# Five edits to a two-block transformer kernel: operand share-out of a chunked recurrence, query order, split sums, constants

## Chip, cores and metric

One core of one Trainium2 chip runs the whole kernel as one program. The metric is device time in microseconds (us) of an execution; three executions of the kernel before gave 2816.89, 2823.05 and 2823.09 us, median 2823.05 us. The core has a matrix engine (TensorE, PE), three elementwise engines (VectorE or DVE, ScalarE or ACT, GpSimd or POOL) and SyncE (SP), which here issues the weight transfers. The engines run side by side and meet at semaphores.

## What is computed

The input is 512 tokens of width 1024. The first block is one hybrid layer, the second has two layers of feed-forward, mixer, feed-forward. Cut to what the change touches:

```python
# first block
h = rms_norm(x, mix_pre_norm) * (1 + sc_m) + sh_m
proj = h @ w_in                       # c_q, c_kv, index keys | r, k, v, decay, a, gate
cq, ckv = rms_norm(c_q, q_norm), rms_norm(c_kv, kv_norm)
y_att = dsa_attention(...)            # causal, 8 heads, top 128 of the latent keys, plus rel. bias
# rwkv7_group, state S (64 x 64) per head, 8 heads, one step per token:
sa = einsum('bhij,bhj->bhi', S, a_t)
S = S * w_t[:, :, None, :] + sa[..., None] * b_t[:, :, None, :] + v_t[..., None] * k_t[:, :, None, :]
y_t = einsum('bhij,bhj->bhi', S, r_t)
x = x + g_m * rms_norm(concat([y_att, y_rwkv]) @ w_out, mix_post_norm)
hf = rms_norm(x, ffn_pre_norm) * (1 + sc_f) + sh_f
x = x + g_f * rms_norm((silu(hf @ w_ffn_gate) * (hf @ w_ffn_up)) @ w_ffn_down, ffn_post_norm)
# second block, two layers
h = h + 0.5 * swiglu(rms_norm_2(h, ...))
h = h + pool_fox_mixer(...)           # layer 0: attention of 8 heads with a forget decay
h = h + mla_mixer(...)                # layer 1: attention of 16 heads, chunk-causal
h = h + 0.5 * swiglu(rms_norm_2(h, ...))
```

Everything is fp32. A dense product is made as three passes over operands that are split into a high and a low part.

## The kernel before

**Stages.** The program is a row of stages, each a block with one instruction list per engine; all engines meet at a stage's end, and POOL then clears the semaphores of that stage (L800) before its own first work of the next. The order is: start; input products (`linear_stage` called with name "inproj", L1626 on); for each of two rounds a recurrence preparation (`rwkv_prep_stage`, L2315) and a recurrence chunk stage (`rwkv_chunk_stage`, L2457); the latent front; attention "dsa"; output product; feed-forward 1 and 2; inputs of the second mixer; attention "fox"; three stages with feed-forwards 3 and 4; attention "mla"; the last feed-forward. Weights come in 1 MB chunks through a ring that SP fills. 97% of the span TensorE is busy, most of it in the dense products.

**Constants.** `keep_clock(pe, bank, n)` (L158) issues n products of the constant identity whose result nobody reads. They stand where TensorE would otherwise wait.

**Input products.** Tiles of 512 tokens by 128 features, 8 pairs of k each (24 products, L748 and L750). Before tile 3, 4, 5, ... a callback puts small work between the tiles: `sums` (L1674) before tile 4 makes column sums of the squares of c_q, c_kv and index keys, 128x1 products from line L782, then four transposes (L1679). ScalarE takes roots of them, and `spread_latents` before tile 5 (L1694) uses those.

**Recurrence.** A round handles two head pairs, called groups 0 and 1. The sequence is cut into 8 chunks of 64. `R.W[g]` are 17 working tiles of 128x512 for each group (`nt, T, TT, X, A, B, K, KH, BH, RT, vt, kht, bht, at, akt, rk, rb`), which the trace names by where they lie (`spare`, `h`, `y`). The preparation stage makes the decays' exponentials on ScalarE, then products of them: on DVE for each group A, B, K and RT (L2448 to L2451), then a copy of the chunk ends (L2452); on POOL KH and BH (L2409, L2410). Its TensorE list ends in products of the adaLN weights (L928), a turn of their rows (L916) and `keep_clock(..., 7)` (14 records of the trace). Its ScalarE list ends in two sigmoids of the gate (round 0 alone).

The chunk stage inverts a triangular 64x64 matrix per chunk by doubling, levels s = 2, 4, 8, 16, 32. `group_steps` lists the steps of one group; the two groups' lists are interleaved. A step is 16 or 32 small products (L2549) and then evacuations on DVE or ScalarE; step n of TensorE waits for all evacuations of the steps up to n-2. Evacuations on DVE: a masked copy of a bank (L2489), `plus_one` (L2496, both inputs in SBUF), `turn` (L2493, a transpose), and the addition of a bank (L2512). The chain of a level is the product nt x T, masked copy X, the product TT x X, addition to T, turn to TT. Into it are put the `extra` steps, which need only the operands: transposes of V, KH, BH, A, then the products K x A, B x RT, K x RT and akt x vt:

```python
            for s in LEVELS[1:]:
                put(full(W.nt, W.T, 0), [("dve", masked(W.X, 0, f"low{s}"))])
                if extra:
                    out.append(extra.pop(0))
```

**Attention** (`attention_stage`, L2116) serves dsa, fox and mla. An item is a head h and a query block i of 128 queries; its scores are (i + 1) x 128 wide. `items` runs over head pairs, in each over the blocks falling (3, 2, 1, 0), in each over the two heads. TensorE works pair of items j: scores of pair j (L2148, in fox also the decay product L2154), transposes of the probabilities of pair j-2 (L2163), products with the values of pair j-3 (L2176 or L782), and `keep_clock(..., 3)` at j = 2 and 3. DVE reduces the scores with the bias or mask (L2206), negates the maximum (L2209), takes the reciprocal and scales (L2218); ScalarE makes the exponentials and copies the transposed probabilities (L2236). In dsa alone POOL makes bias plus mask for each item (L2296, L2295).

**Feed-forwards 1 and 2.** `first_chunks` (L1119) starts with `keep_clock` of 10 or 8 while DVE makes the first features.

## Time and profile before

| | before |
|---|---|
| runs | 2816.89, 2823.05, 2823.09 us |
| profiled execution, own time | 2815.81 us |
| its span | 2814.0 us |
| mean granted clock of TensorE | 0.991 |
| TensorE busy | 2716.2 us, 97%, 16250 instructions |
| VectorE busy | 1312.9 us, 47% |
| ScalarE busy | 847.7 us, 30% |
| GpSimd busy | 563.3 us, 20%, 387 instructions |
| DMA | 248.24 MB, mean 88 GB/s |

The profiled execution's own time is 1.81 us over its span. Times within it are counted from the span's start. In a row of the timeline the first number is the start, the second the length of the group of instructions, and what stands in brackets is the idle time of the engine ahead of it with what ended it. A TensorE row's length holds the drain of its last product, which overlaps the row after it.

### The profile page before, as it was taken

Reading aid. Unit: us, or ns where it says so; the run is one execution under the profiler, and the core shown is the slowest. Engines: PE = TensorE matmul, PEld = TensorE weight load, DVE = VectorE, ACT = ScalarE, POOL = GpSimd, SP = SyncE. Lnnn points to the kernel's source line nnn. Section 1 sums busy time; section 2 is a strip of 40 time slices with the busy share of each in tenths; the row PEclk is TensorE's granted clock in tenths of the full one; section 3 lists DMA queues with packets and bytes.
Section 4 is the critical chain, followed back from the end, with each engine's and each line's share of the span. In section 5 each row is a group of like instructions: output and inputs, shape, how many; then the busy total and the mean of one; then the engine's idle time right before and its main releaser. Section 6 shows DMA issues by size and latency. Waiting matters only on the chain. (4 is left out here: it accounts for less than half of the span.)

```text
span 2814.0 us, 38779 instructions
## 1 busy us (share of the span) xinstructions
PE 2716.2 (97%) x16250; PEld 2175.1 (77%) x16250; DVE 1312.9 (47%) x1851; ACT 847.7 (30%) x1269; POOL 563.3 (20%) x387
## 2 busy tenths in 40 slices
PE   7989898999999999999999999999999999999998
PEld 5868746778888788888868888888888746888886
DVE  3555678453323643335355434354343566543433
ACT  3232135522212421223263212232221347421222
POOL 2000123411212221114101211122021100130202
PEclk9999989999999999999999999999999999999999
DMA  9151210223232233323213232232322240333221
GB/s 291 51 166 48 78 37 5 62 95 98 92 103 84 90 96 98 97 78 107 75 31 105 91 103 92 84 111 91 104 90 90 53 105 1 103 94 104 92 92 42
DMA packets 256942, 248.24 MB, mean 88 GB/s; under 512 B 25972, under 2 KB 252088, under 8 KB 256640
## 3 DMA queue, kind: packets, MB, share of 16 engines
q1 hardware_dynamic: 256562, 245.70, 28.0%
q8 instruction: 129, 2.11, 0.3%
q14 instruction: 45, 0.37, 0.0%
q10 hardware_dynamic: 206, 0.06, 0.0%
HBM read 241.52 MB, written 2.12 MB: 87 GB/s over the span
## 5 line engine op out<-in xcount | busy, mean ns | idle before, releaser
L537 DVE TENSOR_TENSOR dense_wt_lo<-ring,dense_wt_hi 128x2048 fp32r<-128x2048 f32 (+1 forms) x177 | 437.0, 2469 | 290.2 <-ACT dense_wt_hi L522 290.2
L522 ACT CAST dense_wt_hi<-ring 128x2048 fp32r<-128x2048 f32 (+1 forms) x177 | 328.2, 1854 | 758.7 <-PE bank L764 752.7
L1276 POOL TENSOR_TENSOR dense_act_hi<-dense_act,const 128x512 fp32r<-128x512 f32 x110 | 212.9, 1936 | 1306.6 <-DVE dense_act L1268 1306.6
L764 PE MATMUL bank<-feat_hi,dense_wt_hi 128*128 128x512 f32 x1344 | 414.6, 390 | 0.0
L764 PE MATMUL bank<-feat_hi,dense_wt_lo 128*128 128x512 f32 x1344 | 413.8, 389 | 0.0
L764 PE MATMUL bank<-feat_lo,dense_wt_hi 128*128 128x512 f32 x1344 | 413.7, 389 | 0.0
L764 PEld LDWEIGHTS bank<-feat_hi,dense_wt_hi 128*128 128x128 f32 x1344 | 252.3, 188 | 53.3 <-issue 1.0
L764 PEld LDWEIGHTS bank<-feat_hi,dense_wt_lo 128*128 128x128 f32 x1344 | 252.3, 188 | 52.4
L764 PEld LDWEIGHTS bank<-feat_lo,dense_wt_hi 128*128 128x128 f32 x1344 | 252.3, 188 | 52.4
L764 PE MATMUL bank<-dense_act_hi,dense_wt_hi 128*128 128x512 f32 x912 | 281.5, 390 | 1.0 <-POOL dense_act_lo L1278 1.0
L764 PE MATMUL bank<-dense_act_hi,dense_wt_lo 128*128 128x512 f32 x912 | 280.8, 389 | 0.0
L764 PE MATMUL bank<-dense_act_lo,dense_wt_hi 128*128 128x512 f32 x912 | 280.8, 389 | 0.0
L764 PEld LDWEIGHTS bank<-dense_act_hi,dense_wt_hi 128*128 128x128 f32 x912 | 170.6, 188 | 38.4 <-POOL dense_act_lo L1278 3.1
L764 PEld LDWEIGHTS bank<-dense_act_lo,dense_wt_hi 128*128 128x128 f32 x912 | 171.2, 188 | 35.6
L764 PEld LDWEIGHTS bank<-dense_act_hi,dense_wt_lo 128*128 128x128 f32 x912 | 171.2, 188 | 35.6
L1268 DVE TENSOR_TENSOR dense_act<-dense_silu,bank 128x512 f32<-128x512 f32 x110 | 70.7, 684 | 259.6 <-PE bank L764 258.6
L1243 DVE SCALAR_TENSOR_TENSOR x<-bank,x 128x512 f32<-128x512 f32 x96 | 61.9, 686 | 234.1 <-PE bank L764 234.1
L1197 ACT ACTIVATE dense_silu<-dense_silu 128x512 f32<-128x512 f32 x88 | 54.1, 632 | 384.9 <-DVE dense_silu L1255 384.9
L1255 DVE TENSOR_TENSOR dense_silu<-bank,rs 128x512 f32<-128x512 f32 x86 | 55.4, 686 | 224.3 <-PE bank L764 223.9
L1278 POOL TENSOR_TENSOR dense_act_lo<-dense_act,dense_act_hi 128x512 fp32r<-128x512 f32 x110 | 153.4, 1395 | 16.3 <-issue 0.9
L277 POOL TENSOR_TENSOR h<-h 128x512 f32<-128x512 f32 x30 | 39.2, 1306 | 405.6 <-ACT h L262 404.5
L764 PE MATMUL bank<-last_feat_hi,dense_wt_hi 128*128 128x512 f32 x352 | 108.8, 390 | 0.0
(631 smaller groups left out, 3805.4 us busy)
## 6 DMA issues: line engine op xcount, KB each, us to landing
ring<-in_ffn_w_gate SPq DMA_DIRECT2D x44, 1024.0 KB, 5.4
ring<-in_ffn_w_up SPq DMA_DIRECT2D x44, 1024.0 KB, 5.4
ring<-in_ffn_w_down SPq DMA_DIRECT2D x32, 1024.0 KB, 5.0
ring<-in_ada_w SPq DMA_DIRECT2D x24, 1024.0 KB, 8.3
ring<-in_ffn_w_down SPq DMA_DIRECT2D x16, 768.0 KB, 4.2
ring<-in_w_ffn_gate SPq DMA_DIRECT2D x11, 1024.0 KB, 5.4
ring<-in_w_ffn_up SPq DMA_DIRECT2D x11, 1024.0 KB, 5.4
ring<-in_w_in SPq DMA_DIRECT2D x8, 1024.0 KB, 6.3
```

The costliest lines, as they stand in the source:

```text
L277: K.nc.gpsimd.tensor_tensor(K.h[:, 0, :], K.h[:, 0, :], K.h[:, k, :], ALU.add)
L522: self.nc.scalar.copy(self.wh[:, n % 2, 0:words], K.ring[:, n % RING, 0:words]).then_inc(K.high_done, 1)
L537: self.nc.vector.tensor_tensor(self.wl[:, n % 2, 0:words], K.ring[:, n % RING, 0:words], self.wh[:, n % 2, 0:words].bitcast(F32), ALU.subt ...
L764: lasts[m] = pe.matmul(outs[m], a, b, start=n == 0 and p == 0, stop=end and p == 2)
L1197: nc.scalar.activation(g[:, m, :], g[:, m, :], ACT.Silu).then_inc(s_silu, 1)
L1243: v.scalar_tensor_tensor(to, bank, 0.5, to, ALU.mult, ALU.add).then_inc(s_free, 1)
L1255: v.tensor_tensor(g[:, m, :], g[:, m, :] if post and c == 0 else K.bank[m][:, :], K.rs[:, :], ALU.mult).then_inc(s_gate, 1)
L1268: v.tensor_tensor(a[:, m, :], g[:, m, :], K.bank[2 + m][:, :], ALU.mult).then_inc(s_act, 1)
L1276: nc.gpsimd.tensor_tensor(ah[:, f, :], a[:, i % 2, :], K.k("ones")[:, 0:1].broadcast_to([P, T]), ALU.mult)
L1278: nc.gpsimd.tensor_tensor(al[:, f, :], a[:, i % 2, :], ah[:, f, :].bitcast(F32), ALU.subtract).then_inc(s_al, 1)
```

## The change

1. `first_chunks` (L1122): 12 constants in place of 10 (feed-forward 1), and 14 in place of 8 (feed-forward 2).
2. Input products: `sums` keeps the 8 column products of the squares of c_q, before tile 4; a new function `more_sums` does the other 8 and the four transposes, in the middle of tile 4, after 4 of its 8 pairs of k.
3. `attention_stage`: the first head pair takes its query blocks rising (0, 1, 2, 3); all others fall as before. All three attentions.
4. Recurrence. KH and BH are made by POOL at the start of the chunk stage (both KH, then both BH), with a new semaphore `s_hat` on which TensorE waits ahead of their transposes. The preparation has no POOL work left. K and RT are made by DVE in level 4 of the chunk stage, K after the masked copy, RT after the turn. The exponentials are kept for that in tiles rk, rb and akt. The `extra` steps stand in another order: V and A directly after the first two pairs of steps, KH at the end of level 2, BH at the end of level 4, and the four products in levels 8 and 16. The two sigmoids of the gate are moved to the start of ScalarE's list of the chunk stage.
5. The end of the preparation has `keep_clock(..., 2)` in place of 7.

```diff
-            K.keep_clock(pe, K.bank[0], 10 if mix else 8)
+            K.keep_clock(pe, K.bank[0], 12 if mix else 14)
...
-                product3(pe, bank_of(t), tiles[t][4](S, pe, w, t == 0)).then_inc(K.tiles_done, 1)
+                pairs = list(tiles[t][4](S, pe, w, t == 0))
+                if t in extra.get("mid_tensor", {}):
+                    product3(pe, bank_of(t), pairs[:4], stop=False)
+                    extra["mid_tensor"][t]()
+                    product3(pe, bank_of(t), pairs[4:], start=False).then_inc(K.tiles_done, 1)
+                    continue
+                product3(pe, bank_of(t), pairs).then_inc(K.tiles_done, 1)
...
     def sums():
         pe.wait_ge(box["sq"], 4)
-        for at, tiles_in in ((0, (0, 1)), (4, (2,)), (8, (3,))):
+        for b in range(TB):
+            product(pe, K.bank[7][:, b:b + 1], [(sq[n][:, b * P:(b + 1) * P], K.k("ones")[:, 0:1]) for n in (0, 1)])
+
+    def more_sums():
+        for at, tiles_in in ((4, (2,)), (8, (3,))):
...
-    items = [(h + e, i) for h in range(0, H, 2) for i in reversed(range(TB)) for e in range(2)]
+    items = [(h + e, i) for h in range(0, H, 2) for i in (reversed(range(TB)) if h else range(TB)) for e in range(2)]
...
-                K.keep_clock(pe, K.bank[1], 7)
+                K.keep_clock(pe, K.bank[1], 2)
...
-                if rnd == 0:
-                    nc.scalar.activation(M.g[:, :], M.g[:, :], ACT.Sigmoid)
-                    nc.scalar.activation(M.g2[:, :], M.g2[:, :], ACT.Sigmoid)
 
             @block.gpsimd
             def _(pool):
-                for e in range(2):
-                    pool.wait_ge(s_keys, e + 1)
-                    pool.wait_ge(s_exp, 4 * e + 4)
-                    nc.gpsimd.tensor_tensor(W[e].KH, key(e), W[e].TT, ALU.mult)
-                    nc.gpsimd.tensor_tensor(W[e].BH, W[e].bht, W[e].TT, ALU.mult)
+                pass
...
                     v.tensor_tensor(W[e].A, W[e].at, W[e].T, ALU.mult)
-                    v.tensor_tensor(W[e].B, W[e].bht, W[e].nt, ALU.mult)
-                    v.tensor_tensor(W[e].K, key(e), W[e].nt, ALU.mult)
-                    v.tensor_tensor(W[e].RT, M.rkv[:, p, :], W[e].X, ALU.mult)
-                    v.tensor_copy(R.end[:, e, :], chunks(W[e].X)[:, :, C - 1])
+                    v.tensor_tensor(W[e].B, W[e].bht, W[e].rk, ALU.mult)
+                    v.tensor_copy(R.end[:, e, :], chunks(W[e].rb)[:, :, C - 1])
...
-            for src, dst in ((V, W.vt), (W.KH, W.kht), (W.BH, W.bht), (W.A, W.at)):
+            for src, dst in ((V, W.vt), (W.A, W.at), (W.KH, W.kht), (W.BH, W.bht)):
...
+            out.append(extra.pop(0))
+            out.append(extra.pop(0))
             for s in LEVELS[1:]:
-                put(full(W.nt, W.T, 0), [("dve", masked(W.X, 0, f"low{s}"))])
-                if extra:
+                late = []
+                if s == 4:
+                    late = [("dve", lambda: v.tensor_tensor(W.K, key, W.rk, ALU.mult)),
+                            ("dve", lambda: v.tensor_tensor(W.RT, query, W.rb, ALU.mult))]
+                put(full(W.nt, W.T, 0), [("dve", masked(W.X, 0, f"low{s}"))] + late[0:1])
+                if s in (8, 16):
                     out.append(extra.pop(0))
...
+        hat = {2 * at + g: 2 * m + g + 1 for m, at in enumerate((6, 9)) for g in range(2)}
...
+                    if n in hat:
+                        pe.wait_ge(s_hat, hat[n])
...
             def _(pool):
+                for e, W in enumerate(R.W):
+                    nc.gpsimd.tensor_tensor(W.KH, M.rkv[:, 4 + ps[e], :], W.akt, ALU.mult).then_inc(s_hat, 1)
+                for W in R.W:
+                    nc.gpsimd.tensor_tensor(W.BH, W.bht, W.akt, ALU.mult).then_inc(s_hat, 1)
                 pool.wait_ge(s_pe, n_A)
...
             def _(act):
+                if rnd == 0:
+                    nc.scalar.activation(M.g[:, :], M.g[:, :], ACT.Sigmoid)
+                    nc.scalar.activation(M.g2[:, :], M.g2[:, :], ACT.Sigmoid)
```

Lines shift: after the change the small products of the chunk stage are L2560, the masked copies L2491, the turns L2495, `plus_one` L2498, the attention's scores L2159 and transposes L2174.

**Order on POOL, preparation and chunk stage of the first round.** L2409 and L2410 are KH and BH of the kernel before; L800 are the clears. Before:

```order
L800 ISA x27
L2404 UNCONDITIONAL_BRANCH
L2409 TENSOR_TENSOR spare<-rkv,spare 128x512
L2410 TENSOR_TENSOR spare<-spare 128x512
L2409 TENSOR_TENSOR spare<-rkv,y 128x512
L2410 TENSOR_TENSOR spare<-h,y 128x512
L2329 UNCONDITIONAL_BRANCH
L800 ISA x17
L2568 UNCONDITIONAL_BRANCH
L2572 TENSOR_TENSOR spare<-const,end 128x512 x2
```

And with the change, where L2582 is KH and L2584 BH:

```order
L800 ISA x27
L2412 UNCONDITIONAL_BRANCH
L800 ISA x16
L2579 UNCONDITIONAL_BRANCH
L2582 TENSOR_TENSOR spare<-rkv,spare 128x512
L2582 TENSOR_TENSOR spare<-rkv,h 128x512
L2584 TENSOR_TENSOR spare<-spare 128x512
L2584 TENSOR_TENSOR spare<-h 128x512
L2587 TENSOR_TENSOR spare<-const,end 128x512 x2
```

The four products stand behind the branch into the chunk stage and behind its clears (L800), no longer ahead of them.

**Order on DVE, level 4 of the chunk stage of the first round.** L2489 (L2491) is the masked copy, L2512 (L2520) the addition to T, L2493 (L2495) the turn; `spare` and `h` or `y` are groups 0 and 1. Before:

```order
L2489 TENSOR_TENSOR spare<-bank,const 128x512
L2489 TENSOR_TENSOR y<-bank,const 128x512
L2512 TENSOR_TENSOR spare<-bank,spare 128x512
L2493 STREAM_TRANSPOSE spare<-spare 128x512
L2512 TENSOR_TENSOR h<-bank,h 128x512
L2493 STREAM_TRANSPOSE y<-h 128x512
```

With the change, L2514 is K and L2515 RT:

```order
L2491 TENSOR_TENSOR spare<-bank,const 128x512
L2514 TENSOR_TENSOR spare<-rkv,spare 128x512
L2491 TENSOR_TENSOR y<-bank,const 128x512
L2514 TENSOR_TENSOR spare<-rkv,y 128x512
L2520 TENSOR_TENSOR spare<-bank,spare 128x512
L2495 STREAM_TRANSPOSE spare<-spare 128x512
L2515 TENSOR_TENSOR spare<-rkv,spare 128x512
L2520 TENSOR_TENSOR h<-bank,h 128x512
L2495 STREAM_TRANSPOSE y<-h 128x512
L2515 TENSOR_TENSOR h<-rkv,y 128x512
```

Each masked copy is now followed by a K, and each turn by an RT, before the other group's evacuation comes to its turn.

**Order on TensorE, start of the attention mla.** L2148 (L2159) are scores, L2163 (L2174) transposes, L2176 (L2187) products with the values, L158 constants. Before:

```order
L2148 MATMUL bank<-mK,mQ 128x512 x2
L2148 MATMUL bank<-mK,mQ 128x384 x2
L2148 MATMUL bank<-mK,mQ 128x256 x2
L158 MATMUL bank<-const 128x128 x3
L2163 MATMUL bank<-const,mla_S 128x128 x8
L2148 MATMUL bank<-mK,mQ 128x128 x2
L158 MATMUL bank<-const 128x128 x3
L2163 MATMUL bank<-const,mla_S 128x128 x6
L2176 MATMUL bank<-mla_pt,mV 64x128 x8
L2148 MATMUL bank<-mK,mQ 128x512 x2
```

With the change:

```order
L2159 MATMUL bank<-mK,mQ 128x128 x2
L2159 MATMUL bank<-mK,mQ 128x256 x2
L2159 MATMUL bank<-mK,mQ 128x384 x2
L158 MATMUL bank<-const 128x128 x3
L2174 MATMUL bank<-const,mla_S 128x128 x2
L2159 MATMUL bank<-mK,mQ 128x512 x2
L158 MATMUL bank<-const 128x128 x3
L2174 MATMUL bank<-const,mla_S 128x128 x4
L2187 MATMUL bank<-mla_pt,mV 64x128 x2
L2159 MATMUL bank<-mK,mQ 128x512 x2
L2174 MATMUL bank<-const,mla_S 128x128 x6
```

The first transposes are 2 in place of 8, and the widest items of the first head pair stand next to those of the second.

## Rows read from the trace of the kernel before

**Rows 1.** the page, busy time of each engine.

```profile
PE 2716.2 (97%) x16250; PEld 2175.1 (77%) x16250; DVE 1312.9 (47%) x1851; ACT 847.7 (30%) x1269; POOL 563.3 (20%) x387
```

**Rows 2.** view of waits, TensorE: us in total, times, longest us.

```profile
PE bank L2549 <- DVE spare L2493: 7.8, 10, 1.5
...
PE bank L2163 <- ACT mla_pt L2236: 4.5, 15, 0.8
PE bank L2163 <- ACT fox_pt L2236: 4.3, 7, 0.7
```

**Rows 3.** timeline of TensorE, start stage and input products.

```profile
34.47 1.95 PE L782 MATMUL bank<-const,h 128*128 128x1 f32 x16 [0.25 <-POOL h L195]
...
74.50 2.74 PE L782 MATMUL bank<-const,y 128*128 128x1 f32 x24
...
79.43 0.63 PE L748 MATMUL bank<-inproj__feat_lo,inproj_wt_hi 128*128 128x512 f32 x1
...
82.84 0.39 PE L748 MATMUL bank<-inproj__feat_hi,inproj_wt_hi 128*128 128x512 f32 x1
83.06 0.39 PE L748 MATMUL bank<-inproj__feat_lo,inproj_wt_hi 128*128 128x512 f32 x1
```

**Rows 4.** windows: us, busy times and counts by engine, PEclk, DMA share, GB/s.

```profile
80.00:84.00 4.00, 4.00 (x14) 3.16 (x13) 0.00 (x0) 0.00 (x0) 0.00 (x0) 0.65 0.00 0
...
202.00:206.00 4.00, 3.90 (x80) 3.91 (x82) 1.42 (x3) 0.30 (x1) 0.00 (x0) 0.57 0.02 4
```

**Rows 5.** timeline of DVE, end of the first preparation stage.

```profile
187.08 1.75 DVE L2449 TENSOR_TENSOR spare<-spare 128x512 f32<-128x512 f32 x1
...
190.44 0.68 DVE L2451 TENSOR_TENSOR spare<-rkv,spare 128x512 f32<-128x512 f32 x1
...
193.60 0.16 DVE L959 TENSOR_TENSOR mod<-bank,par 128x16 f32<-128x16 f32 x1
```

**Rows 6.** timeline of TensorE, into the first chunk stage.

```profile
189.53 1.18 PE L916 MATMUL bank<-const,rprep_row 128*128 128x1 f32 x8
190.57 1.81 PE L158 MATMUL bank<-const 128*128 128x128 f32 x14
194.14 4.07 PE L2549 MATMUL bank<-spare 64*64 64x64 f32 x128 [1.76 <-PEq L2329]
199.72 1.15 PE L2549 MATMUL bank<-spare 64*64 64x64 f32 x32 [1.51 <-DVE spare L2493]
202.09 1.85 PE L2549 MATMUL bank<-h 64*64 64x64 f32 x32 [1.23 <-DVE y L2493]
```

**Rows 7.** timeline of POOL, same stretch.

```profile
184.89 1.72 POOL L2410 TENSOR_TENSOR spare<-spare 128x512 f32<-128x512 f32 x1
```

**Rows 8.** timeline of attention dsa: TensorE, POOL, DVE.

```profile
442.11 3.25 PE L2148 MATMUL bank<-ckv,h 128*128 128x512 f32 x8 [2.08 <-PEq L1885]
...
443.66 5.92 POOL L2296 TENSOR_TENSOR dsa_bm<-rkv,mask 128x512 f32<-128x512 f32 x6 [30.56 <-issue]
...
465.15 2.62 POOL L2296 TENSOR_TENSOR dsa_bm<-rkv,mask 128x512 f32<-128x512 f32 x2 [1.63 <-DVE dsa_stat L2209]
...
462.88 0.92 DVE L2218 TENSOR_SCALAR dsa_S<-dsa_S,dsa_stat 128x512 f32<-128x512 f32 x2
...
465.21 2.77 DVE L2218 TENSOR_SCALAR dsa_S<-dsa_S,dsa_stat 128x384 f32<-128x384 f32 x2
```

**Rows 9.** timeline of DVE, first chunk stage.

```profile
198.17 0.69 DVE L2496 TENSOR_TENSOR spare<-spare,const 128x512 f32<-128x512 f32 x1
```

**Rows 10.** timeline of TensorE, start of attention mla.

```profile
2302.28 1.09 PE L2163 MATMUL bank<-const,mla_S 128*128 128x128 f32 x8 [0.52 <-DVE mla_S L2218]
...
2305.30 1.00 PE L2163 MATMUL bank<-const,mla_S 128*128 128x128 f32 x6 [0.81 <-ACT mla_pt L2236]
```

**Rows 11.** timeline of TensorE, starts of feed-forwards 1 and 2.

```profile
563.36 0.70 PE L774 MATMUL bank<-feat_hi,dense_wt_hi 128*128 128x512 f32 x2 [1.17 <-DVE feat_lo L478]
...
939.77 1.19 PE L774 MATMUL bank<-feat_hi,dense_wt_hi 128*128 128x512 f32 x2 [2.30 <-DVE feat_lo L665]
```

More of the change, by code:

```diff
@@ L1792, in in_proj_stage @@
                  extra={"sems": sems, "box": box, "sync": sync, "before": before, "helper": helper, "pool": on_pool,
+                        "mid_tensor": {4: more_sums},
                         "at_tensor": {3: ik_product, 4: sums, 5: spread_latents, 6: spread_ik, 7: lambda: dots(0), 8: lambda: dots(1)},
@@ L2323, in rwkv_prep_stage @@
         root, oka = st.sb("root", [P, 2, 8]), st.sb("oka", [P, 2])
-        s_w, s_lora, s_dots, s_sig, s_kk, s_sq, s_norm, s_root, s_inv, s_spread, s_l, s_exp, s_keys = st.sems(
-            "w", "lora", "dots", "sigmoid", "kk", "square", "norm", "root", "inverse", "spread", "logs", "exp", "keys")
+        s_w, s_lora, s_dots, s_sig, s_kk, s_sq, s_norm, s_root, s_inv, s_spread, s_l, s_exp = st.sems(
+            "w", "lora", "dots", "sigmoid", "kk", "square", "norm", "root", "inverse", "spread", "logs", "exp")
         key = lambda e: M.rkv[:, 4 + ps[e], :]
@@ L2357, in _ @@
                     for b in range(TB):
-                        last = pe.matmul(K.bank[4 * e + 3][:, 2 * b:2 * b + 2], W[e].akt[:, b * P:(b + 1) * P], pick, start=True, stop=True)
+                        last = pe.matmul(K.bank[4 * e + 3][:, 2 * b:2 * b + 2], W[e].X[:, b * P:(b + 1) * P], pick, start=True, stop=True)
                     last.then_inc(s_norm, 1)
@@ L2377, in _ @@
                     act.wait_ge(s_kk, e + 1)
-                    nc.scalar.activation(W[e].akt, W[e].at, ACT.Square).then_inc(s_sq, 1)
+                    nc.scalar.activation(W[e].X, W[e].at, ACT.Square).then_inc(s_sq, 1)
                 mod.row_out(act, at)
@@ L2394, in _ @@
                     nc.scalar.activation(W[e].T, W[e].T, ACT.Exp).then_inc(s_exp, 1)
[L2395 to L2397 removed]
+                    nc.scalar.activation(W[e].rk, W[e].kht, ACT.Exp, scale=-1.0).then_inc(s_exp, 1)
+                    nc.scalar.activation(W[e].rb, W[e].kht, ACT.Exp).then_inc(s_exp, 1)
+                    nc.scalar.activation(W[e].akt, W[e].akt, ACT.Exp).then_inc(s_exp, 1)
                 for r in range(at + 3, at + 8):
                     mod.row_out(act, r)
[L2400 to L2402 removed]
             @block.gpsimd
             def _(pool):
[L2406 to L2410 removed]
+                pass
             @block.vector
@@ L2419, in _ @@
                 for e in range(2):
-                    lw, L, eA, eC = W[e].vt, W[e].kht, W[e].T, W[e].TT
+                    lw, L, eA, eC = W[e].vt, W[e].kht, W[e].T, W[e].akt
                     dve.wait_ge(s_sig, 2 * e + 1)
@@ L2444, in _ @@
                     v.scalar_tensor_tensor(W[e].bht, W[e].at, -1.0, W[e].bht, ALU.mult, ALU.mult)
-                    dve.drain().then_inc(s_keys, 1)
+                dve.drain()
                 for e, p in enumerate(ps):
@@ L2463, in rwkv_chunk_stage @@
         S = st.sb("state", [P, 2, 2, HD])
-        s_pe, s_dve, s_act, s_sp, s_sv, s_diag = st.sems("products", "vector_out", "scalar_out", "state_product", "state", "diagonal")
+        s_pe, s_dve, s_act, s_sp, s_sv, s_diag, s_hat = st.sems("products", "vector_out", "scalar_out", "state_product", "state", "diagonal", "scaled_to_end")
         v, a = nc.vector, nc.scalar
@@ L2469, in group_steps @@
             W, b0 = R.W[g], 4 * g
-            V = M.rkv[:, 8 + ps[g], :]
+            V, key, query = M.rkv[:, 8 + ps[g], :], M.rkv[:, 4 + ps[g], :], M.rkv[:, ps[g], :]
             bank = lambda n: K.bank[b0 + n][:, :]
@@ L2506, in group_steps @@
             extra.append((g, full(W.akt, W.vt, 3), [("act", lambda: a.copy(W.akt, bank(3)))]))
+            out.append(extra.pop(0))
+            out.append(extra.pop(0))
             for s in LEVELS[1:]:
-                put(full(W.nt, W.T, 0), [("dve", masked(W.X, 0, f"low{s}"))])
-                if extra:
+                late = []
[4 more added lines that the diff above has]
+                if s in (8, 16):
                     out.append(extra.pop(0))
                 if s != LEVELS[-1]:
-                    put(full(W.TT, W.X, 1), [("dve", lambda: v.tensor_tensor(W.T, bank(1), W.T, ALU.add)), ("drain", None), ("dve", turn(W.TT, W.T))])
+                    put(full(W.TT, W.X, 1), [("dve", lambda: v.tensor_tensor(W.T, bank(1), W.T, ALU.add)), ("drain", None), ("dve", turn(W.TT, W.T))] + late[1:2])
                 else:
                     put(full(W.X, W.TT, 2), [("dve", lambda: v.tensor_tensor(W.TT, bank(2), W.TT, ALU.add))])
-                if extra:
+                if s != LEVELS[-1]:
                     out.append(extra.pop(0))
```

3 lines of the change are left out of this document (removed).

## The prediction

> **What bounds the kernel now.** I read the page first: TensorE is busy 2716.2 of 2814.0 us [rows 1], so only time in which it stands still or runs slowly can be had, some 98 us in all. The view of TensorE's waits comes second. The two places that the change rewrites are there: in the recurrence's chunk stage it waits 7.8 us in 10 waits for a tile of DVE, in the attentions 4.5 us in 15 waits (mla) and 4.3 us in 7 (fox) for ScalarE's copies of the probabilities [rows 2]. Third, the timeline of TensorE at each edited place, with the granted clock by windows, and last DVE and POOL at the same times. The change is hence five small terms, each some us of 2820.
>
> **The base.** The profiled execution's own time is 2815.81 us, near the lowest of the three runs (2816.89, 2823.05, 2823.09); its span is 2814.0. Those four executions have a mean of 2819.7, and I set the sum against that. 0.3% of the median, 8.5 us, is about what a measurement can tell from no change.
>
> **Input products.** Ahead of tile 4 stands an unbroken run of one-column products, from 74.50 to the next dense product. From 79.43 to 82.84 eight dense products start 0.43 us apart, and from there 0.22 [rows 3]; the clock granted in that window is 0.65 as a mean [rows 4], so the lower of the two levels, 1.2 GHz, came behind the run. That costs 8 x 0.2 = 1.6 us. A shorter run of 1.95 us at 34.47 had no such fall behind it. The change leaves runs of about 1.8 and 2.3 us with 12 dense products (2.7 us) between. I take the fall as gone and pay one more break between dense and narrow work, 0.4: **-1.2**. Ends: -1.6, and +0.4 if the clock falls all the same. The roots on ScalarE begin some 2.7 us later; they need to be back for the callback ahead of tile 5, with 12 dense products behind the sums instead of 24, and this hides them, by a narrow margin; if not, TensorE waits under 1 us there.
>
> **End of the preparation.** The chunk stage starts on TensorE at 194.14; DVE had ended with the adaLN addition at 193.60 + 0.16 [rows 5, 6]. DVE's B takes 1.75 while POOL's product (1.72) runs, and 0.68 when POOL is done [rows 5, 7]. With POOL's four products and DVE's K and RT gone, DVE is no longer last: A and B for both groups and two small copies are under 3 us from 185.6. Next late is TensorE itself: the turn at 189.53 is followed by constants at 190.57 [rows 6], of which a few (0.7 us) stay, so it ends near 191.25 and the new stage starts 0.35 later, as now, at 191.6. That is -2.55 a round, **-5.1** for two. The constants dropped cost nothing, they lay under DVE's work; kept, they would now stand on the path. The two sigmoids move off ScalarE's end; in the chunk stage its first copy, of V, is wanted only after the first DVE evacuations, so they lie beside other work.
>
> **K and RT on DVE.** Four operations of 0.68 us [rows 5] come into level 4 of each round, where TensorE already waits for DVE [rows 2]. K stands ahead of the other group's masked copy and RT ahead of its addition to T; of the four, two are on the chain from one group's step to the next: 2 x 0.65 = 1.3 a round, **+2.6**. Ends: 0 and +5.4.
>
> **POOL at the start of the chunk stage.** POOL first clears the sixteen semaphores of the preparation. In dsa, with 22 to clear, its first product came at 443.66, 1.55 after TensorE's first at 442.11 [rows 8]; here I take 1.55 x 16/22 = 1.1. It then holds four products of about 1.7 [rows 7], to some 8 us after the stage's start. In that time DVE does both `plus_one`, 0.69 alone [rows 9], with both inputs in SBUF. By the pair 0.68 and 1.75 [rows 5] that is up to +1.07 each. Group 1's is partly covered by group 0's products, so I take 0.9 a round, **+1.8**; ends 0 and +4.3. KH is wanted only after level 2 and BH after level 4, later than POOL has them, so the two new waits on `s_hat` cost nothing. The new V and A steps behind the first two pairs do not fill the first pause: step n waits for all evacuations up to n-2, and V of group 0 has ahead of it the turn of group 0.
>
> The Trainium skill ("SBUF — State Buffer", section Who interferes with whom) says that a DVE instruction with two SBUF inputs contends with a GpSimd one that reads SBUF, and that whoever issues first blocks the other fully, not in part. By it `plus_one` would wait out a POOL product or slip in ahead of it. It speaks against this part of the change, and the trace agrees in size (1.75 beside 1.72). By the pair of rows this term is +1.8; by the rule, an estimate, each round costs between 0 (`plus_one` gets in first) and 1.7 (it waits out one product), so 0 to +3.4 and a sum of -7.6 to -4.2.
>
> **Clock in the chunk stage.** The pauses behind the first steps are 1.51 and 1.23 [rows 6]. The clock of 202 to 206 was 0.57 in round 1 [rows 4], and a row of 32 products took 1.85 there against 1.15 at 199.72 [rows 6]. The longer pauses (about 2.4 and 1.4) can bring such a fall in both rounds and for longer: 0 to +2.1, I take the middle, **+1.0**. The recurrence together: -5.1 + 2.6 + 1.8 + 1.0 = **+0.3**.
>
> **Attentions.** With the first head pair rising, the first softmax is of 128 columns and no longer 512. In mla the fill has pauses of 0.52 and 0.81 [rows 10], and the first period two of 0.3 [rows 2], 1.9 in all. A pause costs more than its bracket: the row ahead counts the drain of its last product (0.39 long, the next 0.22 later [rows 3]), 0.17 for each of four. 2.6 in all, less one pause of 0.4 that I expect to stay where two blocks of 512 meet: **-2.2**. The work inside is the same, only later. Fox: a like fill (1.3), two waits of 0.61 [rows 2], the drains 0.7, less 0.6 that stays: **-2.6**. Ends for each: 0 and -3.8. In dsa another engine paces it: DVE's scaling takes 2.77 for two tiles of 384 while POOL's bias of 2.62 runs, and 0.92 for two of 512 without [rows 8]. POOL starts at 443.66 whatever the order. What is saved in the fill waits there again: **-0.1**, ends 0 and -2.7.
>
> **Constants of feed-forwards 1 and 2.** TensorE waits 1.17 and 2.30 for the first feature there [rows 11]. Two calls more (0.2) and six more (0.7) lie under those: **0**. The higher clock that they may keep is eaten by DVE's pace of features, for which TensorE waits anyway. Were the cover gone, they would cost 0.9.
>
> **Sum.** -1.2 + 0.3 - 0.1 - 2.2 - 2.6 + 0 = -5.8. On 2819.7 that is **2813.9**; on the profiled time 2810.0, on the median 2817.3.
>
> **Rivals.**
> 1. *The attention's gain is absorbed* as in dsa: the long blocks of heads 0 and 1 now meet those of 2 and 3, and DVE gets behind by what the fill had saved. For it: DVE and ScalarE, not TensorE, end the waits [rows 2]. Against: in mla the pauses in the steady part are only 0.3. Sum -1.2 + 0.3 - 0.1 = -1.0, so 2818.7. Chance 0.22.
> 2. *Everything pays.* POOL and DVE miss each other, K and RT fall into DVE's idle time, no clock falls (recurrence -5.1), in-proj -1.6, dsa -2.7, the others as above: -14.2, 2805.5; with a partial overlap 2805 to 2810. For it: DVE is busy only 47%. Against: in level 4 it is just what TensorE waits for. Chance 0.2.
> 3. *The slower side: POOL meets K and RT.* If POOL starts late or takes longer than 1.7, its last BH still runs when DVE comes to level 4. Then the four take 1.75 in place of 0.68, on the path +4.3 a round on top of the 1.3, and both `plus_one` the full 1.07, and BH is late for TensorE as well. Recurrence: -5.1 + 2 x (1.3 + 4.3 + 2.1 + 1.0) = +12.3. With the attention's gain 2826.2, without 2831. It decides from the point at which POOL's last product ends after DVE's first K. Against: 8 us after a start at 191.6 is before any level 4 (about 204). Chance 0.08.
> 4. *It does not do what it says*: the two runs of sums still halve the clock. That is inside the range, +1.6.
>
> **How the numbers follow.** Forecast 0.5 (own range 2809 to 2819, a bit over half of it below 2814.6, the 0.3% bound), rival 1 0.22, rival 2 0.2, rival 3 0.08. Faster by over 0.3%: 0.26 + 0.19 = 0.45. Slower by over 0.3% (above 2831.5): half of rival 3 and a rest, 0.05. Within 0.3%: 0.50. The range, 2805 to 2822, holds the forecast, rival 1 and most of rival 2, and leaves out rival 3 and the lowest part of rival 2.
>
> **What would show it.** Right: dense products of tile 4 at 0.22 throughout; the chunk stage's first TensorE row about 2.5 earlier than the preparation's own work would place it now; `plus_one` of group 0 longer than 1.5; a wait for the masked copy or addition in level 4; second head pair's first scores of mla 3 us earlier against the stage's start, the whole stage 2 to 3 shorter; dsa no shorter. Wrong: fox and mla of the same length (rival 1); `plus_one` at 0.69 and level 4 without a wait (rival 2); K or RT over 1.2 us (rival 3).

## The result, and the profile after

The change made the kernel slower. Its four executions gave 2835.26 to 2840.66 us, median 2837.61; the kernel before, with one further execution, has a median of 2821.26. The ratio is 1.0049, with a 95% interval of 1.0032 to 1.0066, some 14 us (9 to 19). The forecast was 2813.9 with a range of 2805 to 2822. Of all executions below only one stands apart, 5859.54 us in e7 beside eleven others of 2810.39 to 2828.53; e7's median of 2816.77 counts it (2816.46 without it), its ratio does not, and its cause is not known.

The page of the changed kernel, span and busy times [rows 1]:

```profile
span 2838.8 us, 38774 instructions
...
PE 2733.3 (96%) x16246; PEld 2189.0 (77%) x16246; DVE 1307.3 (46%) x1851; ACT 848.9 (30%) x1269; POOL 558.7 (20%) x387
```

TensorE is busy 17 us longer with hardly more work to do, and the span is 25 us longer. That is more than the 14 us by the ratio: this trace is of the slowest of the four executions (2840.66), and the one of before is of a fast one (2815.81). The view of TensorE's waits (us in total, times, longest) [rows 2]:

```profile
PE bank L684 <- DVE h L679: 9.0, 2, 4.9
PE bank L2560 <- DVE spare L2495: 7.8, 8, 2.3
...
PE bank L2560 <- DVE y L2495: 5.1, 8, 1.2
...
PE bank L2174 <- ACT mla_pt L2247: 3.5, 13, 0.4
PE bank L2174 <- ACT fox_pt L2247: 3.4, 5, 0.8
...
PE bank L2560 <- DVE h L2515: 2.0, 2, 1.0
PE bank L2560 <- DVE spare L2515: 2.0, 2, 1.0
...
PE bank L2560 <- DVE spare L2514: 1.4, 4, 0.5
```

The second longest line of before's attentions is smaller now (4.5 to 3.5 and 4.3 to 3.4). The waits for K and RT (L2514, L2515) are new. And at the top stands a wait that the prediction does not know at all: L684, two times, 9.0 us. To see where the time went I cut both timelines of TensorE at the rows that wait for the stage's branch, and compare each stage with itself, by starts:

| stage | before | after | difference |
|---|---|---|---|
| start | 40.66 | 43.56 | +2.9 |
| input products | 124.88 | 124.93 | 0.0 |
| preparation, round 0 | 28.60 | 27.11 | -1.5 |
| chunk stage, round 0 | 72.06 | 77.62 | +5.6 |
| preparation, round 1 | 26.30 | 29.30 | +3.0 |
| chunk stage, round 1 | 71.05 | 76.40 | +5.4 |
| latent front | 78.56 | 79.67 | +1.1 |
| dsa | 59.43 | 58.78 | -0.7 |
| output product | 52.57 | 52.58 | 0.0 |
| feed-forwards 1 and 2 | 750.08 | 750.28 | +0.2 |
| inputs of the second mixer | 102.17 | 108.73 | +6.6 |
| fox | 51.73 | 49.36 | -2.4 |
| three stages, feed-forwards 3 and 4 | 798.29 | 805.46 | +7.2 |
| preparation of mla | 40.59 | 40.54 | 0.0 |
| mla | 94.47 | 91.97 | -2.5 |
| last feed-forward | 422.56 | 422.51 | -0.1 |

Three groups stand out: the attentions -5.5, the recurrence's four stages +12.4, and +13.7 in two stages that the change was not thought to touch. The start, whose code is the same in both, differs by 2.9, the latent front by 1.1.

**The two waits at L684.** TensorE's timeline at the start of the second mixer's inputs, before and then after:

```profile
1304.19 2.25 PE L158 MATMUL bank<-const 128*128 128x128 f32 x18 [1.42 <-PEq L833]
1306.20 0.48 PE L748 MATMUL bank<-feat_hi,abin_wt_hi 128*128 128x512 f32 x1
...
1310.84 1.02 PE L684 MATMUL bank<-h,const 128*128 128x512 f32 x2
```

```profile
1320.23 2.25 PE L158 MATMUL bank<-const 128*128 128x128 f32 x18 [1.42 <-PEq L833]
1326.58 2.05 PE L684 MATMUL bank<-h,const 128*128 128x512 f32 x2 [4.10 <-DVE h L679]
1327.64 1.42 PE L748 MATMUL bank<-feat_hi,abin_wt_hi 128*128 128x512 f32 x1
1328.85 0.63 PE L748 MATMUL bank<-feat_lo,abin_wt_hi 128*128 128x512 f32 x1
```

Before, constants were followed by 20 dense products of the first tile (L748, L750), and the product L684, which sums the squares for the norm, came as the 21st, when its operand was there. Now L684 comes first, waits 4.10 us, and the next dense products behind it start 0.43 us apart in place of 0.23: the granted clock from 1326.58 to 1330.98 is 0.50, its lower level. This is the instruction order of the program, not chance. The order of TensorE there, before:

```
L158 MATMUL bank<-const 128x128 x9
L748 MATMUL bank<-feat_hi,abin_wt_hi 128x512
L748 MATMUL bank<-feat_lo,abin_wt_hi 128x512
...
L748 MATMUL bank<-feat_lo,abin_wt_hi 128x512
L684 MATMUL bank<-h,const 128x512
L750 MATMUL bank<-feat_hi,abin_wt_lo 128x512
```

and after:

```
L158 MATMUL bank<-const 128x128 x9
L684 MATMUL bank<-h,const 128x512
L748 MATMUL bank<-feat_hi,abin_wt_hi 128x512
L748 MATMUL bank<-feat_lo,abin_wt_hi 128x512
```

What did it is the one word `list` in the diff. The pairs of a tile come from a generator (L1456), and drawing a pair calls `S.feature(pe, k, wait)` (L718), which issues the wait for feature k and, at the last k, the whole of `deferred_sum` (L681). `product3` drew them one at a time, between the products. `pairs = list(...)`, meant for the one tile that is split, draws all of them ahead of the first product, and does so for every tile of every `linear_stage`. So the first tile waits for all eight features and for the sum of squares. The inputs of the first block don't pay, since their first two tiles go another way.

**The chunk stage.** TensorE, DVE and POOL of round 0 (answers to [rows 5, 6, 7, 9]):

```profile
194.29 0.87 PE L158 MATMUL bank<-const 128*128 128x128 f32 x4
195.60 5.19 PE L2560 MATMUL bank<-spare 64*64 64x64 f32 x128 [0.44 <-PEq L2340]
203.09 1.15 PE L2560 MATMUL bank<-const,rkv 64*64 64x64 f32 x32 [2.30 <-DVE spare L2495]
205.46 1.98 PE L2560 MATMUL bank<-const,rkv 64*64 64x64 f32 x32 [1.22 <-DVE y L2495]
...
223.08 1.15 PE L2560 MATMUL bank<-const,spare 64*64 64x64 f32 x32 [1.01 <-DVE spare L2515]
225.25 1.88 PE L2560 MATMUL bank<-const,spare 64*64 64x64 f32 x32 [1.02 <-DVE h L2515]
```

```profile
194.47 0.17 DVE L959 TENSOR_TENSOR mod<-bank,par 128x16 f32<-128x16 f32 x1 [3.90 <-PE bank L916]
...
200.61 1.62 DVE L2498 TENSOR_TENSOR spare<-spare,const 128x512 f32<-128x512 f32 x1
...
203.91 0.69 DVE L2498 TENSOR_TENSOR h<-h,const 128x512 f32<-128x512 f32 x1
...
218.80 0.68 DVE L2514 TENSOR_TENSOR spare<-rkv,spare 128x512 f32<-128x512 f32 x1
```

```profile
196.72 1.27 POOL L2582 TENSOR_TENSOR spare<-rkv,spare 128x512 f32<-128x512 f32 x1 [71.70 <-issue]
...
200.42 1.26 POOL L2584 TENSOR_TENSOR spare<-h 128x512 f32<-128x512 f32 x1
```

The preparation's DVE is done early and its adaLN addition, at 194.47, waits for TensorE's turn: it no longer sets the end. POOL's first product comes 1.12 after TensorE's first. `plus_one` of group 0 takes 1.62 beside POOL's last product, that of group 1, when POOL is done, 0.69. The pause behind the first two pairs is 2.30 (before 1.51), the next 1.22. In level 4 there are two of 1.0 for RT. And the clock: windows of the start and of the last three of the recurrence's stages (columns: us, busy times, PEclk, DMA share, GB/s), before and after:

```profile
0.00:40.66 40.66, 25.16 (x238) 16.42 (x239) 4.41 (x12) 12.52 (x24) 7.82 (x10) 1.00 1.03 333
194.14:266.20 72.06, 62.70 (x1897) 59.97 (x1897) 36.36 (x64) 10.55 (x18) 2.05 (x2) 0.98 0.09 28
266.20:292.50 26.30, 23.27 (x257) 15.57 (x257) 21.08 (x39) 13.52 (x26) 6.32 (x4) 1.00 0.77 251
292.50:363.55 71.05, 61.32 (x1897) 58.60 (x1897) 36.36 (x64) 10.55 (x18) 2.05 (x2) 1.00 0.10 30
```

```profile
0.00:43.56 43.56, 27.89 (x238) 18.30 (x239) 4.40 (x12) 12.43 (x24) 7.82 (x10) 0.92 1.00 320
...
195.60:273.22 77.62, 65.34 (x1896) 62.14 (x1897) 39.64 (x68) 12.95 (x21) 7.00 (x6) 0.94 0.11 34
273.22:302.52 29.30, 27.02 (x246) 18.36 (x247) 15.38 (x35) 13.74 (x26) 0.00 (x0) 0.79 0.64 209
302.52:378.92 76.40, 64.96 (x1896) 61.96 (x1897) 38.71 (x68) 10.56 (x18) 7.01 (x6) 0.95 0.11 34
```

The granted clock was 1.00, 0.98, 1.00, 1.00 and is 0.92, 0.94, 0.79, 0.95. A pause in itself, and the slow products behind it, both count.

**Sums in two runs.** The window in which before had 0.65 [rows 4] has 1.00 now, and the next one has the fall (windows after, same columns):

```profile
80.00:84.00 4.00, 4.00 (x30) 3.63 (x28) 0.00 (x0) 0.00 (x0) 0.00 (x0) 1.00 0.00 0
84.00:88.00 4.00, 4.00 (x15) 3.19 (x14) 0.33 (x2) 0.57 (x3) 0.00 (x0) 0.68 0.00 0
```

**Attention.** TensorE at the start of mla (answers to [rows 10]):

```profile
2324.32 2.88 PE L2159 MATMUL bank<-mK,mQ 96*128 96x128 f32 x12 [0.95 <-PEq L2942]
...
2327.71 0.38 PE L2174 MATMUL bank<-const,mla_S 128*128 128x128 f32 x2
...
2331.21 1.98 PE L2159 MATMUL bank<-mK,mQ 96*128 96x512 f32 x4
...
2336.24 1.06 PE L2174 MATMUL bank<-const,mla_S 128*128 128x128 f32 x8 [0.31 <-ACT mla_pt L2247]
```

No pause is left in the fill; the second head pair's scores of 512 start at 2331.21, 6.89 after the stage's start, and before it was 10.28. One wait of 0.31 stands where the 512 wide blocks meet.

### The profile page after: what moved, and what is told of

It reads as the page before. It is cut to its first block and busy times, and to the rows that moved or that the text cites. A ratio compares the mean times of both kernels' runs of the same rounds, so it can differ in the third digit from the quotient of the medians.

```text
span 2838.8 us, 38774 instructions
## 1 busy us (share of the span) xinstructions
PE 2733.3 (96%) x16246; PEld 2189.0 (77%) x16246; DVE 1307.3 (46%) x1851; ACT 848.9 (30%) x1269; POOL 558.7 (20%) x387
```

## Experiments

Each kernel was timed in five rounds beside the kernel before on the same chip. "e2" and so on are their names. Ratios are to the kernel before.

### e1, the list alone

```diff
-                product3(pe, bank_of(t), tiles[t][4](S, pe, w, t == 0)).then_inc(K.tiles_done, 1)
+                product3(pe, bank_of(t), list(tiles[t][4](S, pe, w, t == 0))).then_inc(K.tiles_done, 1)
```

> The kernel before with one edit: the pairs of a tile are gathered in a list ahead of its products, as the change does for all tiles of linear_stage. Theory L (the list takes the waits and the sum of the deferred norm, which the pairs' generator issues as it is drawn, ahead of the first product of a tile): TensorE waits about 4 us for L679 at the start of the second mixer's inputs and about 5 at the mla inputs, those two stages are 6.5 and 7 us longer, the whole 12 to 14 us slower. Rival (the list is harmless, the longer stages came from the clock or from chance): within 3 us of the kernel before.

Measured: 2837.59 us, ratio 1.0044 (1.0031 to 1.0057), +13.9 against 2823.71 of the kernel before in the same rounds. Its waits:

```profile
PE bank L684 <- DVE h L679: 9.3, 2, 5.2
```

The inputs of the second mixer are 109.28 long (before 102.17), the three stages with the mla inputs 806.19 (798.29). The list is shown to be the cause, and by itself it is as large as the whole difference.

Its windows of start and of the second preparation, stages whose instructions are those of before:

```profile
0.00:45.18 45.18, 28.65 (x238) 18.91 (x239) 4.41 (x12) 12.47 (x24) 7.79 (x10) 0.89 0.96 309
270.80:299.82 29.02, 27.95 (x257) 19.22 (x257) 21.16 (x39) 13.75 (x26) 6.31 (x4) 0.82 0.65 209
```

They are 45.18 and 29.02 long, where the profile of before had 40.66 and 26.30. Over the thirteen later traces the start took 41.0 to 46.8, with no change to its code. The mean granted clock of the start was 0.85 to 0.96 in those thirteen, 1.00 in the trace of before; in the second preparation it was 1.00 in two of the thirteen (e5, e7) and 0.79 to 0.88 in the others. The trace that the prediction rests on was a lucky one, with none of these falls, and its own time (2815.81) had said so against medians of 2821 to 2826.

### e2, the whole change with the list for the split tile alone

```diff
-                pairs = list(tiles[t][4](S, pe, w, t == 0))
+                pairs = tiles[t][4](S, pe, w, t == 0)
                 if t in extra.get("mid_tensor", {}):
+                    pairs = list(pairs)
```

> The whole change, but with the list only for the one tile that is split. Theory L: both waits at L684 are gone and the time is 12 to 14 us below that of the change, so 2824 to 2826, still 2 to 5 us slower than before, all of it from the recurrence. Rival (harmless list): as slow as the change, 2838.

Measured: 2824.96, ratio 1.0002 (0.9991 to 1.0012). The waits of 4 and 5 us are gone (0.26 is left at the second), both stages are back to within 1 us of before. So theory L holds. The 2 to 5 us slower than before that it also expected are not seen: by the interval, what is left of the change lies between 2.5 us faster and 3.4 us slower, nothing that can be told from no change.

### e3, the recurrence alone, and e4, everything but the recurrence

e3 is the kernel before with the diff's parts on `rwkv_prep_stage` and `rwkv_chunk_stage`, e4 is e2 without them:

```diff
# e4 against e2, of the parts taken back
-                K.keep_clock(pe, K.bank[1], 2)
+                K.keep_clock(pe, K.bank[1], 7)
...
-            for src, dst in ((V, W.vt), (W.A, W.at), (W.KH, W.kht), (W.BH, W.bht)):
+            for src, dst in ((V, W.vt), (W.KH, W.kht), (W.BH, W.bht), (W.A, W.at)):
```

> The kernel before with the recurrence's part alone (with its 2 in place of 7 constants). Theory R (what the trace of the change shows in those four stages, +12.4 us): 10 to 13 us slower than before. Rival (chance falls of the clock made most of it): 0 to 5 us slower.

> The change without the recurrence's part and with the list for the split tile alone: query order, sums in two runs, constants. Theory (the attentions pay 5.5 us as their stages show, sums and constants nothing): 5 to 6 us faster than before. Rival (the time saved in a stage is lost by falls of the clock behind it): within 2 us.

Measured: e3 2828.34, ratio 1.0018 (1.0009 to 1.0026), +4.6; e4 2820.16, 0.9991 (0.998 to 1.0002), -3.5. The parts add up: 13.9 + 4.6 - 3.5 = 15.0 against 14 to 16 for the whole, though each part is known only to some 2.4 to 3.7 us either way, and the interval of e4 reaches from 5.6 us faster to 0.6 slower. In e3 I had expected 10 to 13, read from the stages of the one trace; it is 4.6, the rival's value. The four stages take 207.4 in e3's own trace and 210.4 after, 198.0 in before's; but with the same instructions as before's they take 200.7, 202.7 and 203.2 in the traces of e1, e4 and e9. Against those e3 is 4 to 7 longer, which fits its 4.6, and 3 to 5 of the 12.4 us were the lucky trace of before. e4's profile shows the attentions at -0.97, -2.37 and -2.52, the input products at 123.31 (-1.57), and against that +2.04 in the output product behind dsa, where the clock falls now (mean 0.96, before 1.00), and +1.35 in the three stages behind fox. So of 7.4 saved in the stages 4.0 are left, against 3.5 in the medians.

### e5, K and RT made in the preparation again

```diff
                     v.tensor_tensor(W[e].B, W[e].bht, W[e].rk, ALU.mult)
+                    v.tensor_tensor(W[e].K, key(e), W[e].rk, ALU.mult)
+                    v.tensor_tensor(W[e].RT, M.rkv[:, p, :], W[e].rb, ALU.mult)
...
-                if s == 4:
-                    late = [("dve", lambda: v.tensor_tensor(W.K, key, W.rk, ALU.mult)),
-                            ("dve", lambda: v.tensor_tensor(W.RT, query, W.rb, ALU.mult))]
```

> The change with the list for the split tile alone (as e2), and K and RT made in the preparation again, in the 3.9 us in which DVE there waits for TensorE. Theory K (the four operations cost only where TensorE waits for DVE, in level 4): the pauses of 1.0 us before the second half of level 4 fall to 0.45, each chunk stage is 1.8 us shorter, the preparation no longer; with a fall of the clock less, 3 to 7 us below e2. Rival (level 4 waits for the chain anyway, and the clock takes back what is won): within 1.5 us of e2.

Measured: 2819.55, ratio 0.9986 (0.9977 to 0.9996), 5.4 below e2 in the medians and 4.5 by the two ratios (0.5 to 8.5 with their intervals). The waits for L2514 and L2515 are gone from its view of waits, where the longest of the chunk stages are now these:

```profile
PE bank L2560 <- DVE spare L2498: 8.5, 10, 2.0
PE bank L2560 <- DVE y L2498: 6.0, 10, 1.2
```

The chunk stages are 73.24 and 72.92 long, in e2 75.12 and 76.40; the preparations 26.86 and 24.37, not longer than e2's 27.42 and 27.65. So the four operations of 0.69 us are free in the preparation, and in level 4 each chunk stage is 2.7 us longer with them as a mean of these two traces. Theory K holds as to the place. The size is less sure: in e5's first round the pause behind the first two pairs is 1.18 us and in e2's 2.19, since POOL was done there before a late `plus_one`, and that has nothing to do with K and RT.

### e6, the transposes in the old order

```diff
-            for src, dst in ((V, W.vt), (W.A, W.at), (W.KH, W.kht), (W.BH, W.bht)):
+            for src, dst in ((V, W.vt), (W.KH, W.kht), (W.BH, W.bht), (W.A, W.at)):
...
-            out.append(extra.pop(0))
-            out.append(extra.pop(0))
             for s in LEVELS[1:]:
...
-        hat = {2 * at + g: 2 * m + g + 1 for m, at in enumerate((6, 9)) for g in range(2)}
+        hat = {2 * at + g: 2 * m + g + 1 for m, at in enumerate((5, 7)) for g in range(2)}
```

> As e2, but the transposes stand as before: V and KH in level 2, BH and A in level 4, with the waits on s_hat moved along; K and RT still in level 4 on DVE. Theory O (V and A do not fill the pause behind the first two pairs, they only come ahead of the critical product, and levels 2 and 4 lose their cover): each chunk stage 1 us shorter than in e2, the sum 1 to 3 us below e2. Rival (the new order is neutral, TensorE waits in other places for the same sum): within 1 us.

Measured: 2826.41, ratio 1.0014 (1.0003 to 1.0025), against e2's 1.0002. Theory O falls; the chunk stages are 76.70 and 76.66 long, no shorter than e2's 75.12 and 76.40, and the new order is neutral or slightly better. The first pause of round 0 is 2.2 to 2.3 with either; that V and A take from the levels the same work that they bring in front is my reading of the traces and was not tried alone.

### e7, e5 and e6 together, POOL behind both plus_one; e8, with constants in the pauses

```diff
+                pool.wait_ge(s_dve, 7)
                 for e, W in enumerate(R.W):
                     nc.gpsimd.tensor_tensor(W.KH, M.rkv[:, 4 + ps[e], :], W.akt, ALU.mult).then_inc(s_hat, 1)
# e8 only, in TensorE's loop over the steps
+                    if n in (4, 5):
+                        K.keep_clock(pe, K.bank[2], 5 if n == 4 else 3)
```

> e5 and e6 together, and POOL starts KH and BH only when both plus_one are done. What stays of the recurrence's part is that POOL's four products have left the preparation. Theory: chunk stage as before (72.1 and 71.0 without a further fall of the clock), plus_one 0.69 in both rounds, preparation 1 to 2.5 us shorter each; 5 to 8 us below e2, so 1 to 4 below e4 (2817 to 2819). Rival (the shorter preparation brings its time back as falls of the clock): as e4, 2820.

> e7 with five and three constants of TensorE in the two pauses (1.5 and 1.2 us) behind the first two pairs of steps of each chunk stage. Theory C (falls of the clock behind those pauses are a real part of the recurrence's cost): granted clock 1.00 behind them in both rounds, 1 to 3 us below e7. Rival (the falls move elsewhere, or the constants delay the next step): within 1 us of e7 or slower by up to 1.

Measured: e7 2816.77, ratio 0.9983 (0.997 to 0.9996); e8 2816.68, ratio 0.9973 (0.9962 to 0.9985). DVE and POOL of e7's first chunk stage, where L2501 is `plus_one`:

```profile
204.96 0.69 DVE L2501 TENSOR_TENSOR spare<-spare,const 128x512 f32<-128x512 f32 x1
...
207.34 0.69 DVE L2501 TENSOR_TENSOR h<-h,const 128x512 f32<-128x512 f32 x1
```

```profile
208.11 1.27 POOL L2581 TENSOR_TENSOR spare<-rkv,spare 128x512 f32<-128x512 f32 x1 [80.26 <-DVE h L2501]
```

`plus_one` is back at 0.69 and POOL's four products lie behind it; the chunk stages are 72.43 and 71.02 long, as before (72.06, 71.05), with the preparations 0.4 and 2.4 shorter than in before's trace. The intervals of e7 and e4 (0.998 to 1.0002) overlap, so the rival, that e7 is as fast as e4, is not excluded. TensorE in e8's pauses:

```profile
203.94 1.38 PE L158 MATMUL bank<-const 128*128 128x128 f32 x10
205.31 1.15 PE L2560 MATMUL bank<-spare 64*64 64x64 f32 x32
206.39 0.94 PE L158 MATMUL bank<-const 128*128 128x128 f32 x6
207.69 1.15 PE L2560 MATMUL bank<-h 64*64 64x64 f32 x32 [0.36 <-DVE y L2498]
```

The two pauses are filled but for 0.36 (0.20 and 0.36 in the second round), and no fall follows them in either round. But none follows the open pauses in e7's trace either: its granted clock is 1.00 from 204 us on and in all of the second chunk stage. In the medians e7 and e8 are the same, and their intervals overlap; theory C is not shown.

### e9, the rising first head pair alone

> The kernel before with the rising first head pair alone. Theory A (the stages' own savings reach the end): dsa 0.7 to 1.0, fox 2.4 and mla 2.5 us shorter, the whole 4 to 6 us faster. Rival (what dsa saves comes back as a fall of the clock in the output product behind it, 2 us): 2 to 4 us faster.

Measured: 2819.45, ratio 0.9986 (0.9976 to 0.9996), -4.1. The edit is the one line of the diff. Its stages show -0.99, -2.39 and -2.56, and +2.07 in the output product behind dsa. The value lies where the two expectations meet (4 to 6 and 2 to 4), so it does not decide between them; the fall behind dsa is in the trace, as the rival has it.

### e10, e8 without split sums and constants; e11, e8 with seven constants; e12, e10 again

e10 takes back the edits of `first_chunks` and `sums`, e11 the `keep_clock(..., 2)`.

> e8 without the split of the sums and with the feed-forwards' 10 and 8 constants. Theory (the split saves 1.6 us in the executions in which no other fall takes its place, the constants nothing or under 1): 0 to 2 us slower than e8. Rival (both parts are worth nothing): within 0.5 us, not to be told from e8.

> e8 with 7 constants at the end of each preparation again, in place of 2. Theory (they now stand on the path, 0.65 us a call of five per round, since DVE is done before them): 1 to 1.5 us slower than e8. Rival (they keep the clock up at the start of the chunk stage, where e2, e5 and e8 show falls): equal or up to 3 us faster.

> e10 once more, unchanged, to see whether the version that is faster than both kernels holds: rising first head pair; K and RT in the preparation, KH and BH on POOL behind both plus_one, the transposes in the old order, five and three constants in the pauses; no list, no split sums. If e10's 0.9961 holds: 0.995 to 0.9975. Rival (it was a good draw of the clock's falls, five executions only): 0.9975 to 0.999, as e8 and e5.

Measured: e10 2812.47, ratio 0.9961 (0.9947 to 0.9976), five executions; e11 2815.27, 0.997 (0.9959 to 0.9981); e12, the same kernel as e10 in rounds of its own, 2816.97 against 2826.3, ratio 0.9962 (0.9947 to 0.9977). Taking both parts back costs nothing that can be measured; by the intervals of e8 and e10 they could together be worth up to some 2 us. e11 can't be told from e8 either: the 1 to 1.5 us that were expected are less than these runs can tell. e10 with e12 is the version that beats the kernel before by 0.38%, about 11 us, and with it the changed one. The rising first head pair gives 4 of that by itself (e9); the rest is, by elimination, POOL's work out of the preparation with K and RT left there, and the pauses filled, which were not timed apart in this setting.

## Why the prediction was wrong, step by step

**The step that failed: a term was missing.** The part "Input products" costs the split of tile 4 and says nothing of `pairs = list(...)`, so it puts that line at 0 without a reason. The line moved L684 ahead of 20 products in two other stages, where TensorE then waited 4.1 and 4.9 us, and cost +13.9 (e1). With it the sum would have been -5.8 + 13.9, so 2827.8 on 2819.7. That is the largest part of the miss and not all of it: the recurrence came out at +4.6 (e3) against +0.3, and the rest of the change at -3.5 (e4) against -6.1. Together that is +15.0, against the +14 to +16 measured. The rival "it does not do what it says" asked only whether the clock falls behind the sums, and none asked what else goes through the changed line. The new order of TensorE's instructions shows it without any run; I had looked in it only at the places that the diff is about.

**The base.** Setting the sum on 2819.7, a mean of four executions, was sound within a few us (later medians of the kernel before were 2823.2 to 2826.3). What was not sound is that each stage was priced from a trace without falls in the start and the second preparation.

**Input products, -1.2.** Right in the stage where it worked (-1.57 in e4, e8 and e11), nothing in the others (0.0 after, e2, e5, e6, e7): in the trace after, the fall came some five products behind the second run instead. So in five of the eight traces with the split it went as rival 4 has it, and the six without the split have no such saving (124.88 to 124.97).

**End of the preparation, -5.1.** The mechanism is right: DVE is out of the way and TensorE sets the end. Round 0 gave -1.5 after, of the missing 1.1, 0.8 is a longer wait for weights, 1.36 where before it was 0.59. Round 1 gave -1.9 and -2.4 where the clock held (e5, e7), and up to +3.3 where it did not. Against the traces of e1, e4 and e9, whose preparations are as before (28.6 to 30.2 in round 0, 29.0 to 29.6 in round 1), after's are 1.5 to 3.1 shorter in round 0 and within 0.4 of the same length in round 1. What the four products on POOL are worth by themselves, in time of the whole, was not measured.

**K and RT, +2.6.** Under-rated, by how much is open: +4.5 by the ratios of e5 and e2, with 0.5 to 8.5 by their intervals. The pauses of level 4 sum to 2.7 a round (0.47, 0.23, 1.01, 1.02), in e5 to 1.1 (0.68, 0.44), so 1.6 a round and not 1.3, or 3.2 for two. Where the rest comes from is open: the clock means of the chunk stages do not settle it (0.98 and 0.94 in e2, 0.96 and 0.98 in e5), and a part is the shorter first pause in e5's round 0.

**POOL beside `plus_one`, +1.8.** 1.62 for group 0 after and 1.39 and 1.36 in e3's two rounds, 0.69 for group 1: one operation a round, +0.7 to 0.9. In the second round after, where TensorE was slow at the start, POOL was done before and `plus_one` took 0.69. So the term was 0.7 to 1.4. The Trainium skill's rule ("SBUF — State Buffer", Who interferes with whom) fits: POOL's last product began at 200.42 and ran 1.26, to 201.68, and `plus_one`, issued at 200.61, ended 0.55 after that. POOL's products were 1.27 and not 1.7: DVE's masked copies beside them read a bank (in e3 the last one began beside `plus_one` and took 1.71). They were done by 201.7, long before the first K at 218.80, and rival 3's condition never came. (Rival 3's total with the attention's gain adds up to 2825.9 and not 2826.2; nothing hangs on it.)

**Clock in the chunk stage, +1.0.** Under-rated. The clock means fell to 0.94 and 0.95 after. In e3, which has the same instructions in both rounds, the chunk stage took 73.63 at a mean clock of 1.00 and 75.54 at 0.95, so a round with such a fall costs some 2 us. After, the two are 4.0 and 2.8 longer than the 73.63. Recurrence as a whole: +0.3 forecast, +4.6 (2.5 to 7.3 by the interval) measured in e3.

**Attentions, -4.9.** Right, -5.5 in the stages (dsa -0.7, fox -2.4, mla -2.5; forecast -0.1, -2.6, -2.2), and in fox and mla the mechanism as told. dsa was forecast to be no shorter and is; why was not studied. End to end it is -4.1 (e9, 1.1 to 6.8 faster by the interval): in eight of the eleven traces with the rising head pair the output product behind dsa is 2.0 to 2.4 us longer, at a lower clock. Rival 1 is refuted by the stages.

**Constants of the feed-forwards, 0.** As forecast, as far as the traces show; they were timed only together with the split sums (e10). In feed-forward 2 the wait of 2.30 is gone from the trace and the stage is as long as it was (750.28 with feed-forward 1, before 750.08): the constants fill it, and from the next feature on DVE sets the pace as ever. In feed-forward 1 the first wait is 2.25 and not shorter than before's 1.17.

## What to carry to other kernels

A generator that issues instructions as it is drawn is part of the program's order. Gathering it in a list, or drawing it early, moves waits and whole products; after any rewriting of a loop compare the instruction order of every stage that goes through the line, not of the one it is meant for.

Work moved off a stage's end is won only if it lands where its engine is idle and nobody queues behind it: the same four operations were free where DVE waited for TensorE and cost some 4 to 5 us where TensorE waited for DVE.

Before pricing stages from one profile, ask where its own time lies among the runs: the start stage, which has no edit, differed by up to 6 us between traces.

## What the hardware showed that was not expected

A saved pause need not stay saved. In e4 and e9 the attention dsa is 1.0 us shorter, and the output product behind it 2.0 longer at a mean granted clock of 0.96 in place of 1.00, with the same instructions there. Such a fall stands in eight of the eleven traces with the rising head pair and in none of the three without it (52.57, 52.61 and, with a small fall, 53.19 us); this count speaks for the rising order as its cause but does not show it. In the same eight traces the three stages behind fox are 799.0 to 799.6 long, against 797.9 to 798.3 in before, e3, e6 and e10; why the two go together is open. What mla saves stays: the last feed-forward behind it is 422.2 to 422.6 long in every trace. In the start stage, which no kernel changed, the length went from 40.66 with a granted clock of 1.00 to 46.8 in e8.

POOL's product took 1.27 us beside DVE operations that read a bank, and 1.72 in before's preparation beside those that read only SBUF [rows 7]; in e3 it took 1.71 beside `plus_one`.
